# Moving the adds of a sum of squares behind the next block's update, and half a weight split ahead of the squares, in a two-model transformer kernel

## The reference

```
for l in range(DEPTH):
    h  = modulate(rms_norm(x, norm1_g[l]), sh1, sc1)
    hc = modulate(rms_norm(xc, norm1_g[l]), csh1, csc1)
    ...                                   # token mixer on h and hc gives mix
    x = x + g1 * jnp.einsum('blm,md->bld', mix, w_out[l])
    x = x + g2 * swiglu(modulate(rms_norm(x, norm2_g[l]), sh2, sc2),
                        w_ffn_in[l], w_ffn_out[l])
    ...                                   # the same for the context, but not in the last layer

def rms_norm(x, g):
    xf = x.astype(jnp.float32)
    y = xf * lax.rsqrt(jnp.mean(xf * xf, axis=-1, keepdims=True) + EPS)
    return (y * g.astype(jnp.float32)).astype(x.dtype)
```

## Time and profile before

| | |
|---|---|
| time, median of three runs | 2667.32 us (2666.88 to 2670.68) |
| the profiled execution, its own time | 2670.68 us |
| its span, first to last instruction | 2668.9 us |
| TensorE busy, share of the span | 2500.0 us, 94% |
| VectorE | 1333.4 us, 50% |
| ScalarE | 798.2 us, 30% |
| GpSimd | 904.6 us, 34% |
| mean granted clock of TensorE | 0.951 |

### The profile page before, as it was taken

The page is one execution under the profiler, slowest core; times in us unless marked ns, Lnnn a source line. Parts: engine busy times, 40 slices in busy tenths (PEclk is TensorE's granted clock), DMA queues, the critical chain, the costliest instruction groups (busy, mean ns, idle before and its releaser), DMA issues.

```text
span 2668.9 us, 30774 instructions
## 1 busy us (share of the span) xinstructions
PE 2500.0 (94%) x13049; PEld 2044.4 (77%) x13049; DVE 1333.4 (50%) x1700; ACT 798.2 (30%) x1079; POOL 904.6 (34%) x629
## 2 busy tenths in 40 slices
PE   7998789999999999898899999989999989999998
PEld 4788568888888888687677778868887437788886
DVE  2994856645444443875646655654652223311113
ACT  2322652311211112335632122234332333322222
POOL 2331201233333332443034545543442002444442
PEclk9998889899999999898899999989998998999999
DMA  8222012234334242221034545531113001233331
GB/s 265 88 95 96 17 32 64 79 115 125 106 113 127 91 123 87 71 100 52 1 95 130 154 150 158 158 118 48 36 29 111 16 0 43 75 95 88 94 96 63
DMA packets 309225, 240.57 MB, mean 90 GB/s; under 512 B 10692, under 2 KB 304831, under 8 KB 309087
## 3 DMA queue, kind: packets, MB, share of 16 engines
q1 hardware_dynamic: 308674, 238.47, 29.3%
q10 hardware_dynamic: 414, 0.13, 0.0%
HBM read 232.29 MB, written 2.10 MB: 88 GB/s over the span
## 4 chain that ended last, share of the span: by engine, by line
PE 81%; DVE 14%; ACT 3%; issue 1%; DMA 1%; POOL 0%; SPq 0%; DVEq 0%; ACTq 0%
PE ps L2362 56%; PE ps L1097 5%; DVE conv_acc L1024 3%; PE ps L2390 3%; DVE mod_w L2019 2%; PE ps L709 2%; DVE mod_ctx L2019 2%; PE ps L922 1%; PE ps L1117 1%; PE ps L660 1%; DVE small L991 1%; PE ps L2278 1%; PE ps L736 1%; PE ps L1140 1%; PE ps L884 1%
## 5 line engine op out<-in xcount | busy, mean ns | idle before, releaser
L1580 POOL TENSOR_TENSOR w_lo<-raw,w_hi 128x512 fp32r<-128x512 f32 x546 | 811.9, 1517 | 1582.4 <-ACT w_hi L1671 1582.4
L2362 PE MATMUL ps<-h_hi,w_hi 128*128 128x512 f32 x1994 | 644.9, 369 | 35.9 <-DVE h_lo L1983 22.3
L2362 PE MATMUL ps<-h_lo,w_hi 128*128 128x512 f32 x1994 | 640.1, 367 | 0.0
L2362 PE MATMUL ps<-h_hi,w_lo 128*128 128x512 f32 x1994 | 639.1, 366 | 0.0
L1671 ACT ACTIVATE w_hi<-raw 128x2048 fp32r<-128x2048 f32 (+2 forms) x155 | 264.8, 1708 | 653.9 <-PE ps L2362 372.2
L2362 PEld LDWEIGHTS ps<-h_hi,w_hi 128*128 128x128 f32 x1994 | 340.7, 191 | 107.5 <-issue 31.5
L2362 PEld LDWEIGHTS ps<-h_hi,w_lo 128*128 128x128 f32 x1994 | 340.0, 190 | 67.2
L2362 PEld LDWEIGHTS ps<-h_lo,w_hi 128*128 128x128 f32 x1994 | 340.4, 190 | 66.3
L1910 ACT ACTIVATE xg<-ps 128x512 f32<-128x512 f32 (+1 forms) x66 | 44.2, 670 | 678.3 <-PE ps L2362 491.6
L2019 DVE SCALAR_TENSOR_TENSOR mod_w<-mod_w,cond 128x512 f32<-128x512 f32 x224 | 241.7, 1079 | 3.4
L2362 PE MATMUL ps<-hid_hi,w_hi 128*128 128x512 f32 x704 | 231.4, 369 | 0.0
(11 more groups left out here) (359 smaller groups left out, 3225.4 us busy)
## 6 DMA issues: line engine op xcount, KB each, us to landing
mod_w<-in_w_mod SPq DMA_DIRECT2D x72, 1024.0 KB, 9.4
raw<-in_w_ffn_in SPq DMA_DIRECT2D x88, 512.0 KB, 5.3
raw<-in_w_in SPq DMA_DIRECT2D x54, 512.0 KB, 4.8
raw<-in_w_ffn_out SPq DMA_DIRECT2D x48, 384.0 KB, 3.8
raw<-in_w_out SPq DMA_DIRECT2D x24, 512.0 KB, 4.5
raw<-in_w_gate SPq DMA_DIRECT2D x22, 512.0 KB, 4.0
raw<-in_w_up SPq DMA_DIRECT2D x22, 512.0 KB, 5.3
raw<-in_w_down SPq DMA_DIRECT2D x24, 384.0 KB, 3.8
```

Of the source, the lines that this page charges most:

```text
L1580: ins = pool.tensor_tensor(w_lo[:, s, at:end], raw[:, s, at:end], w_hi[:, s, at:end].bitcast(F32), ALU.subtract)
L2362: ins = pe.matmul(ps[0:m, at:at + tw], weight(part, k, cols), v[:, k, t0:t0 + tw], start=(at_k == 0 and j == 0 and not shared), stop=(at_k ...
```

## The change

Three edits, all in the four blocks ahead of norms 1 to 6.

On ScalarE, the squares of block b - 1 come after next_hi of block b, where before the squares of block b came after next_hi of block b. Then the early half of the weight split (early_hi) is issued ahead of the squares of blocks 2 and 3, and no longer behind them. The late piece stays behind them.

On VectorE, the adds into n_acc of block b - 1 come after add_to_x of block b, where before those of block b came after add_to_x of block b (for b = 0, 1) and, for block 2, between the two halves of add_to_x of block 3. The call for block 3 adds nothing, since tiles 6 and 7 are not added. Which tiles are squared, added and summed, and all semaphores, are the same.

```diff
                 for b in range(3):
                     next_hi(n0 + b)
-                    squares_of_block(ni, n0, b)
+                    if b >= 1:
+                        squares_of_block(ni, n0, b - 1)
+                early = n0 + 5 in early_blocks
+                if early:
+                    split_early_hi(n0 + 5)
+                squares_of_block(ni, n0, 2)
                 squares_of_block(ni, n0, 3)
-                if n0 + 5 in early_blocks:
-                    split_early_hi(n0 + 5)
+                if early:
                     split_late_hi(n0 + 5)
...
                     if ni and b == 3 and t == 0:
                         ins.then_inc(n_x, 1)
-                        add_block(ni, 2)
                 ins.then_inc(psum_free[s], 1)
...
                     add_to_x(n, b, l, 16, parts[l], 2 * l + 1)
-                    if b < 2:
-                        add_block(2 * l + 1, b)
+                    if b >= 1:
+                        add_block(2 * l + 1, b - 1)
+                add_block(2 * l + 1, 3)
                 norm(2 * l + 1, (A_N2, A_N2 + 8, A_GF)[l], pairs_saved((l, 9)))
...
                         add_to_x(n, b, l, 40, parts[l], 2 * l + 2 if ends else None)
-                        if g0 + g == HID // P and b < 2:
-                            add_block(2 * l + 2, b)
+                        if g0 + g == HID // P and b >= 1:
+                            add_block(2 * l + 2, b - 1)
+                    if g0 + g == HID // P:
+                        add_block(2 * l + 2, 3)
```

## The result

The changed kernel took 2701.02 us (median of 4 runs, 2697.60 to 2703.41), the kernel before 2669.0 us in the same comparison (4 runs, 2666.88 to 2671.97). The ratio is 1.0119, 95% interval 1.0107 to 1.0133: slower by some 32 us. The forecast was 2692 us with a range of 2675 to 2699. The direction was right, and the time lies 2 us above the range. The execution that was profiled took 2706.74 us, 5.7 above the median.

A forecast was written before the change was run, and what follows sets the result against it. TensorE, 81% of the chain of waits, was taken to lose time at six tails; root shifts of 4.9, 6.8, 2.5, 5.8, 2.35 and 2.9 sum to 25.25 us, giving 2692 us from the 2667.32 median, range 2675 to 2699.

The forecast's parts named there:

- The chain: After the last wide matmul: x, two adds, all 36 or 24 one-column matmuls, then the root; early_hi off the path.
- tails: Ends of six sums of squares: 1, 3, 5 after out-projections of layers 0 to 2, 2, 4, 6 after feed-forwards; +25.25 us.
- S: Start of the one-column matmuls after the last wide matmul, per tail: 3.3, 4.5, 3.0, 5.3, 2.3 and 2.3 us.
- The columns and the clock: TensorE's 36 or 24 one-column summing matmuls: 0.112 us each at 2.4 GHz, 0.21 at 1.2 GHz, clock falling after 4.05 us.
- two ends: Kernel before: clock still high until 2.7 us after the last wide matmul in tail 1, 5.4 us in tail 5.
- covered price: Cost of two adds on VectorE while GpSimd works: 3.84 us at 768 tokens, 2.56 at 512; high end +31.7 us.
- Between the tails: Stretches where TensorE was said to run wide matmuls without pause, so nothing there could take up a delay.
- Cost 0: early_hi on ScalarE ahead of squares 4 to 7: 0 in tail 4, up to 1 us if weights land late.
- clock did not hold: Rival: in the tails the clock falls only once the columns are done; +12.3 us, 2680 us; chance 0.18.
- Full blocking: Rival: each covered add waits out a whole GpSimd piece, a pair 5.2 us; +30, 2697 us; chance 0.10.
- Faster: Rival: adds cost nothing at the tails' ends, only early_hi's exit counts; -3.5 us, 2664 us; chance 0.03.
- no difference: Rival: the tails' shifts are given back later, for instance as later blocks find weights ready earlier; chance 0.04.

The follow-up runs named there:

- adds_back: Changed kernel with the adds of tiles 4 and 5 put back between the two halves of x of block 3: 2677.74 us, ratio 1.0035.
- last_adds: Kernel before with only the adds of tiles 4 and 5 moved behind both halves of x of block 3: 2694.79 us, ratio 1.0087.
- second profile: The changed kernel run and profiled once more, nothing changed: 2700.75 us.
- dve_only: Kernel before with VectorE's edit alone, ScalarE's order kept: 2698.68 us, ratio 1.0106.
- early_only: Kernel before with only early_hi moved ahead of the squares of blocks 2 and 3: 2676.33 us, ratio 1.0024.
- after_quiet2: Changed kernel with GpSimd waiting for all five adds before it makes early_lo: 2698.35 us, ratio 1.0090.
- early_odd2: Kernel before with early_hi ahead of the squares of blocks 2 and 3 only in tails 1, 3 and 5: 2670.65 us, ratio 0.9994.
- after_hold: Changed kernel with 9 to 24 dummy 128x512 matmuls ahead of the columns in TensorE's idle time: 2686.48 us, ratio 1.0062.

## Why the prediction was right in its mechanism and short in its size

*The chain.* Right. The adds of m = 4 and 5 stand behind the last x, TensorE's first column waits for the second of them, and the root waits for the columns. early_hi and the table load have left the chain. It is shown from both sides: by putting the adds back (adds_back, about −22 us) and by moving the adds alone (last_adds, +23 us). One sign was off: early_hi was to start 10 us or more before the last x in tails 1, 3 and 5, and in tails 3 and 5 it started 7.0 and 7.8 us before it.

*S.* Right within 0.6 us in every tail, and 21.95 us for 20.7 in all. Tail 4 missed 0.6 us: its last pair of adds began 1.9 us after the last wide matmul (1804.26 less 1802.35), where 2.4 had been counted, but the pair took 3.86 us, beside GpSimd throughout, and not 2.9 (rows below). Tail 5 missed 0.55 us. The prediction took GpSimd as idle there, but early_lo had moved ahead and ran beside the first add:

```profile
2293.81 4.46 POOL L1564 TENSOR_TENSOR early_lo<-raw,early_hi 128x512 fp32r<-128x512 f32 x4
```

*The columns and the clock: the term that was mis-sized.* The prediction let the clock fall 4.05 us after the last wide matmul in every tail, the middle of two ends. It fell after 2.9, 2.6, 3.5, 5.2, 2.1 and 4.0 us, 3.4 on average. The pitch of a column at the low clock was right (0.21 us, twelve from 490.31 to 492.86). So the columns took 37.55 us and not 33.15, +4.4 us, where S added 1.25. Together 5.65 us, these are, but for rounding, the 5.4 us by which the roots moved further than forecast (30.65 less 25.25); 1.6 of these came back behind the roots and 2.7 were added between the tails. In the second profile, whose time is near the median, the columns took 35.2 us, +2.0, and the roots moved 3.1 us further than forecast, so nearly half of this error belongs to the one execution. The largest errors are in tail 5 (+1.8), tail 1 (+0.95) and tail 3 (+0.8). In tail 1 the fall came 0.35 us before the first column, so all 36 were slow and not 29.

The two ends from which 4.05 was taken were falls with the columns close behind the wide matmuls: 28 or 29 matmuls were in flight up to the fall. (In tail 5 all 24 columns were done, TensorE had then been idle for 2.2 us, and the first transposes had begun.) In the new tails TensorE is idle first. That an idle TensorE loses its clock sooner is not shown: the fall came on average 4.3 us after the last wide matmul before and 3.4 in the first profile of the changed kernel, but 3.8 in its second one, 4.0 in last_adds and 4.4 in dve_only, where TensorE is idle first as well. What should have been done is plain without it: a term that hangs on a point that varies by 3 us should have been summed at both ends for each tail, and the high end of these sums was near.

*The range.* Its high end was +31.7 us on the median of 2667. By its words it had every column slow and every pair at the covered price. Its numbers do not: for tails 1, 5 and 6 they hold the price beside an idle GpSimd (2.0 and 1.45 us). With 3.84 and 2.56 us there the sum is about 36 us, and the range ends at 2703, above the measured 2701. In tail 5 that omission was real: the pair took 1.85 us. Two more things were left out. One is where the sum starts: 2667.3 was the median of three runs, and the kernel before measured 2669.0 to 2671.6 in all later comparisons, so the forecast itself began 2 to 4 us low. The other is what lies between the tails. The second profile gives the account of a usual execution: roots +28.3, behind the roots −1.3, between the tails +3.5, ahead of tail 1 −0.4, together +30.1 us on the profile of before, whose execution took 2670.68 us.

*Between the tails.* The prediction said that TensorE runs wide matmuls there without pause, so that nothing there could take up a delay, and gave no term. That reading holds for the first and the last of the five stretches. In the three others TensorE was busy for 270.4 of 297.0, 381.5 of 391.4 and 448.8 of 473.0 us before the change. The five stretches from tail 1 to tail 6 summed to 2108.9 us before, 2108.3 in dve_only and 2108.0 in last_adds, which have ScalarE's list as before. They summed to 2111.6 and 2112.4 in the changed kernel's two profiles, 2112.0 in early_only, 2112.3 in after_quiet2 and 2114.1 in adds_back, which all have early_hi ahead, and to 2110.9 in early_odd2, which has it ahead in three tails. So ScalarE's edit seems to cost some 3 us there. after_hold, with early_hi ahead and dummies, has only 2109.9, and one and the same stretch varied by up to 5 us among these kernels. That makes early_only's 6.4 us whole: 3.3 in the tails and 3.1 between them. Which wait it is was not found, and each sum is from a single profile.

*early_hi.* Cost 0, the prediction said, up to 1 us if the weights land late. It waited 0.86 us in tail 4, 0.51 in tail 3 and 0.44 in tail 5. The landing was placed well: early_hi was to end 0.4 us after the last wide matmul and ended 0.5 us after it (1802.88 and 1802.35). It was harmless only because the adds had moved behind x; with the adds where they were, the same edit costs 4.3 us in that tail (early_only).

*The rivals.* The clock did not hold: after_hold shows what holding it is worth, 14 to 15 us, where the prediction's two cases lay 12 us apart (2692 and 2680). Full blocking put a pair at 5.2 us; the slowest pair on the path took 3.86 us, and the pair of tail 2 took 2.94:

```profile
1082.43 2.94 DVE L1960 TENSOR_TENSOR n_acc<-n_acc,sq 128x768 f32<-128x768 f32 x2
...
1804.26 3.86 DVE L1960 TENSOR_TENSOR n_acc<-n_acc,sq 128x768 f32<-128x768 f32 x2
```

It falls for the adds. Its 2697 us was nearer to the measured time than the forecast, but that is luck: the missing time was in other terms. *Faster* and *no difference* fall too.

The parts in one line, each from a kernel of its own: the adds behind the last x +23 us; with the earlier adds moved too, that is all of VectorE's edit, +28; all three edits +32. Inside these, the low clock is 14 to 15 us. These are differences of medians with intervals of some 3 us either way, so the 5 and the 4 between them are rough: in the profiles, the tails of dve_only are only 1.7 us longer than those of last_adds.

So the step of the prediction that failed is the term for the columns, with one fall of the clock at 4.05 us for all six tails: 33.15 us were counted, and 37.55 and 35.2 us measured. The time left the range because its high end did not hold what its words say, because it began at a low median, and because it had no term for the stretches between the tails, whose cause stays open.

## What to carry to other kernels

Where a reduction ends a phase, look at which operation stands last on the engine that feeds it: two adds of 1 us, moved behind the last input, cost 1.5 to 7.3 us a tail here (last_adds, 23 us in six tails), because all of the summing stood behind them and then ran at half the clock. Price the work behind a new idle gap at both clock levels, tail by tail, and keep both for the range. Moving work to an earlier place on one engine needs a look at whom its successors now meet: early_hi's move sent GpSimd's memsets under a copy on the path, and squares behind a DMA.

## What the runs showed of the hardware

A copy on VectorE stood out two whole memsets of GpSimd. n_wide (128x768) takes 0.57 us alone, and took 0.77 us beside early_lo in tail 2 of the kernel before:

```profile
1076.70 0.77 DVE L1976 COPY n_wide<-n_root 128x768 f32<-128x768 f32 x1
```

Beside the memsets of u_pool and u_conv it took 3.18 us in early_only, and the same in dve_only, here VectorE's row and then GpSimd's:

```profile
1090.54 3.36 DVE L1976 COPY n_wide<-n_root 128x768 f32<-128x768 f32 x1
```
```profile
1090.67 1.43 POOL L1604 MEMSET u_pool<- 128x1600 f32 x1
1092.04 1.46 POOL L1605 MEMSET u_conv<- 128x1626 f32 x1
```

The copy ended 0.4 us after the second memset (1093.90 and 1093.50). The adds behaved otherwise: beside GpSimd's early_lo or w_lo one of 768 took up to 1.95 us for 0.96 alone. The Trainium skill (SBUF — State Buffer, "Who interferes with whom") says that a copy on VectorE in its mode of two ports and GpSimd keep each other out for a whole instruction. No row names the mode; the copy's 0.57 us, where an add of the same size takes 0.96, fits it. The trace of the copy agrees, except that it shows the copy, which began 0.13 us ahead of the first memset, as the one that lasts.

Columns did not keep the clock. In tail 1 of the kernel before TensorE ran them without a gap from the last wide matmul on, and the clock fell in their midst, 2.6 us after that matmul. Wide matmuls with no use of their own kept it: with 13 to 24 of them in the gap, 36 columns took 4.2 to 5.4 us instead of 7.8. Begun only after the fall, seven such matmuls took 3.33 us and delayed what stood behind them.
